# Making the Strassen sums of down's weights early, in DRAM

## The reference

```python
h = rmsnorm(x, mix_norm_g)
proj = h @ w_in                       # q, k, v (16 heads of 128) and 16 forget logits
q, k = rmsnorm(q, g_q), rmsnorm(k, g_k)
c = cumsum(log_sigmoid(f_logit + b_f))
logit[t, s] = q[t] . k[s] / sqrt(128) + c[t] - c[s]      # for s <= t
x = x + (softmax(logit) @ v) @ w_out
h = rmsnorm(x, ffn_norm_g)
gate, up = split(h @ w_gate_up)       # 2 x 5632 columns
x = x + (silu(gate) * up) @ w_down    # 5632 x 2048
```

## Time and profile before

| | before |
|---|---|
| median of 3 runs | 2136.73 us (2135.73 to 2136.99) |
| the profiled execution | 2136.44 us, span of its records 2134.7 us |
| PE busy | 2113.3 us (99%) |
| DVE busy | 1526.2 us (71%) |
| ACT busy | 944.6 us (44%) |
| DMA | 376.31 MB, 176 GB/s over the span |

### The profile page before, as it was taken

One profiled execution on the slowest core, in us unless ns is written; L12 is line 12 of the kernel. 1 busy time (PEld: TensorE's weight loads), 2 busy tenths in 40 slices (PEclk: granted clock), 3 DMA queues, 4 the chain that ended last, 5 costly groups with the idle time before them and its releaser, 6 DMA issues. The chain is left out here.

```text
span 2134.7 us, 27909 instructions
## 1 busy us (share of the span) xinstructions
PE 2113.3 (99%) x10404; PEld 1845.4 (86%) x10404; DVE 1526.2 (71%) x2108; ACT 944.6 (44%) x1281; POOL 174.2 (8%) x354
## 2 busy tenths in 40 slices
PE   8999999999999999999999999999999999999998
PEld 8999999999998888888888888888888777887876
DVE  4444444444455435888888987987978998999999
ACT  5333333333343335444444444544445554544533
POOL 0322222222221000000000000000000000000000
PEclk9999999999999999999999999999999999999999
DMA  6232333232243344666666666676677877868766
GB/s 185 76 99 79 93 85 92 79 98 79 84 128 128 119 134 132 198 218 200 219 212 211 208 219 212 204 233 204 198 235 232 269 256 246 263 208 269 260 186 203
DMA packets 258924, 376.31 MB, mean 176 GB/s; under 512 B 15842, under 2 KB 114180, under 8 KB 258324
## 3 DMA queue, kind: packets, MB, share of 16 engines
q1 hardware_dynamic: 255456, 354.90, 52.8%
q10 hardware_dynamic: 3380, 20.21, 2.5%
HBM read 346.45 MB, written 28.61 MB: 176 GB/s over the span
## 5 line engine op out<-in xcount | busy, mean ns | idle before, releaser
L1391 DVE TENSOR_TENSOR f_lo<-f_raw,f_hi 128x1536 fp32r<-128x1536 f32 (+1 forms) x230 | 454.4, 1980 | 46.9 <-ACT f_hi L1020 31.4
L564 PE MATMUL gemm<-w_hi,act_t 128*128 128x384 f32 (+2 forms) x1280 | 450.7, 352 | 2.3 <-DVE w_lo L1207 2.3
L565 PE MATMUL gemm<-w_lo,act_t 128*128 128x384 f32 (+2 forms) x1280 | 443.9, 347 | 0.0
L566 PE MATMUL gemm<-w_hi,act_t 128*128 128x384 f32 (+2 forms) x1280 | 443.9, 347 | 0.0
L765 PE MATMUL gemm<-f_hi,a_form 128*128 128x512 f32 x1056 | 411.2, 389 | 0.0
L767 PE MATMUL gemm<-f_hi,a_form 128*128 128x512 f32 x1056 | 411.1, 389 | 0.0
L766 PE MATMUL gemm<-f_lo,a_form 128*128 128x512 f32 x1056 | 410.8, 389 | 0.0
L765 PE MATMUL aux<-f_hi,a_form 128*128 128x512 f32 x792 | 313.2, 395 | 6.7 <-DVE f_lo L1391 5.1
L1207 DVE TENSOR_TENSOR w_lo<-w_raw,w_hi 128x768 fp32r<-128x768 f32 (+1 forms) x160 | 160.7, 1008 | 208.5 <-ACT w_hi L862 208.5
L766 PE MATMUL aux<-f_lo,a_form 128*128 128x512 f32 x792 | 308.5, 390 | 0.0
L767 PE MATMUL aux<-f_hi,a_form 128*128 128x512 f32 x792 | 308.5, 390 | 0.0
(11 more groups left out here) (184 smaller groups left out, 2227.5 us busy)
## 6 DMA issues: line engine op xcount, KB each, us to landing
f_raw<-in_ffn_w_gate_up SPq DMA_DIRECT2D x264, 512.0 KB, 4.2
f_raw<-in_ffn_w_down SPq DMA_DIRECT2D x132, 512.0 KB, 4.8
w_raw<-in_fox_w_in SPq DMA_DIRECT2D x192, 256.0 KB, 3.3
f_raw<-in_ffn_w_gate_up SPq DMA_DIRECT2D x88, 256.0 KB, 4.0
w_raw<-in_fox_w_out SPq DMA_DIRECT2D x16, 1024.0 KB, 5.1
f_raw<-in_ffn_w_down SPq DMA_DIRECT2D x44, 256.0 KB, 4.9
a_raw<-forms_scratch SPq DMA_DIRECT2D x22, 512.0 KB, 6.6
forms_scratch<-fa_a ACTq DMA_DIRECT2D x11, 896.0 KB, 6.3
```

Of the source, the lines that this page charges most:

```text
L564: mm(out, a_hi, b_hi, start=first, stop=False)
L565: mm(out, a_hi, b_lo, start=False, stop=False)
L566: return mm(out, a_lo, b_hi, start=False, stop=last)
L1391: v.tensor_tensor(f_lo[:, n % 4, 0:3 + g], f_raw[:, n % 4, 0:3 + g], f32(f_hi[:, n % 3, 0:3 + g]), ALU.subtract).then_inc(f_lo_done, 1)
```

## The change

The four blocks of every g = 1 unit of down are now loaded in the heads stage, summed there by DVE and stored in a DRAM tensor `t_scratch`. In down the units load the finished sums, and DVE's three instructions are gone; ACT's `f_hi` then waits for the load alone.

Heads 2 to 12 (`PRE_FIRST` to `PRE_END` - 1, a `Fori` of their own) each handle four units u = 0 to 3 of 1 MB. They use two buffers: `pre_w` behind `w_hi` for u = 0 and 2, `pre_rows` in the last quarter of `rows` for u = 1 and 3. ACT issues the loads (two DMAs each) and the stores (one DMA). A load waits until the buffer's last store has landed, a store until DVE's sums are made, DVE's sums until both halves of the load have landed. `add_p1` in down has one more wait.

```diff
+        pre = [at("pre_w", AREA_W + 49152, [P, 4, CW]), at("pre_rows", AREA_S + 24576, [P, 4, CW])]
@@ SP, the loads of the FFN's units
-                else:
+                elif r < R_DOWN:
                     for half in range(2):
                         sp.dma_start(f_raw[:, s, 2 * half:2 * half + 2], src[:, half, :, col:col + CW])\
                             .then_inc(f_ld[s], 16)
+                else:
+                    if r == R_DOWN and j == 0:
+                        for b in range(2):
+                            sp.wait_ge(pre_stored[b], 16 + 16 * NSTEP)
+                    made = dram_t[PRE_FIRST + step // 2, step % 2, (r - R_DOWN) % 2]
+                    for half in range(2):
+                        sp.dma_start(f_raw[:, s, 2 * half:2 * half + 2], made[:, 2 * half:2 * half + 2])\
+                            .then_inc(f_ld[s], 16)
@@ ACT
+            def load_blocks(h, u):
+                act.wait_ge(pre_stored[u % 2], 32 * (h - PRE_FIRST) + 16 * (u // 2) + 16)
+                src = w_down_v[bass.ds(h - PRE_FIRST, 1), u // 2].rearrange("o p r c x -> (o p) r c x")
+                for r in range(2):
+                    act.dma_start(pre[u % 2][:, 2 * r:2 * r + 2], src[:, r, :, u % 2 * CW:(u % 2 + 1) * CW])\
+                        .then_inc(pre_ld[u % 2], 16)
+
+            def store_sums(h, u):
+                act.wait_ge(pre_step, 12 * (h - PRE_FIRST) + 3 * u + 3)
+                dst = dram_t[bass.ds(h, 1), u // 2, u % 2].rearrange("o p f x -> (o p) f x")
+                act.dma_start(dst, pre[u % 2][:]).then_inc(pre_stored[u % 2], 16)
@@ in_chunk on ACT, in the order of a slot s
+                    if sums and s in (0, 1, 8):
+                        load_blocks(h, {0: 0, 1: 1, 8: 2}[s])
                     ...
+                    if sums and s == 10:
+                        load_blocks(h, 3)
                     ...
+                    if sums and s in (5, 8, 13, 14):
+                        store_sums(h, {5: 0, 8: 1, 13: 2, 14: 3}[s])
@@ ACT, f_hi of a g = 1 unit
-                    act.wait_ge(t_step, 3 * T_COUNT[n] + 1)
+                    if r < R_DOWN:
+                        act.wait_ge(t_step, 3 * T_COUNT[n] + 1)
+                    else:
+                        act.wait_ge(f_ld[n % 4], LANDED[n])
@@ DVE
+            def pre_sums(h, u):
+                f = pre[u % 2]
+                dve.wait_ge(pre_ld[u % 2], 64 * (h - PRE_FIRST) + 32 * (u // 2) + 32)
+                ...
+                v.tensor_tensor(f[:, 0:2], f[:, 0:2], f[:, 1:4:2], ALU.add).then_inc(pre_step, 1)
+                ...
+                v.tensor_tensor(f[:, 3], f[:, 0], f[:, 3], ALU.add).then_inc(pre_step, 1)
+                ...
+                v.tensor_tensor(f[:, 2], f[:, 3], f[:, 2], ALU.add).then_inc(pre_step, 1)
@@ in_chunk on DVE, in slot s behind split_lo
+                    if sums and s in (4, 7, 11, 12):
+                        pre_sums(h, {4: 0, 7: 1, 11: 2, 12: 3}[s])
@@ DVE in down
-                sums = n + 2 < NU and UNITS[n + 2][1] == 1
+                sums = n + 2 < NU and UNITS[n + 2][1] == 1 and UNITS[n + 2][0] < R_DOWN
```

More of the change, by code:

```diff
@@ L91, in encoder_layer @@
     dram_forms = nc.dram_tensor("forms_scratch", (NSTEP, P, 7, HW), F32, kind="Internal").ap()
+    PRE_FIRST, PRE_END = 2, 2 + FF // CW
+    dram_t = nc.dram_tensor("t_scratch", (PRE_END, 2, 2, P, 4, CW), F32, kind="Internal").ap()
     dram_x1 = nc.dram_tensor("x1_scratch", (ND, P, NT, CW), F32, kind="Internal").ap()
@@ L238, in encoder_layer @@
         f_ld = [sem(f"f_loaded{s}") for s in range(4)]
+        pre_ld, pre_stored = [sem("pre_loaded0"), sem("pre_loaded1")], [sem("pre_stored0"), sem("pre_stored1")]
+        pre_step = sem("pre_step")
         t_step, f_hi_done, f_lo_done = sem("t_step"), sem("f_hi_done"), sem("f_lo_done")
@@ L319, in encoder_layer @@
         assert len(SPLIT_NTH) == 2 * NSTEP
+        w_down_v = w_down.rearrange("(g r i p) (c x) -> g i p r c x", r=2, i=2, p=P, c=2)
         block = ctx.enter_context(nc.Block())
@@ L385, in _ @@
             w_gu_v = w_gu.rearrange("(g r i p) (c x) -> g i p r c x", r=2, i=2, p=P, c=2)
-            w_down_v = w_down.rearrange("(g r i p) (c x) -> g i p r c x", r=2, i=2, p=P, c=2)
             def load_forms(b, g, j):
@@ L928, in heads_hi, with in_chunk @@
                              rows_flat[:, h0 * S:(h0 + n) * S], ACT.Copy).then_inc(oT_hi_done, 1)
-            def in_chunk(h, second=False, last=False):
+            def load_blocks(h, u):
[8 more added lines that the diff above has]
+                act.dma_start(dst, pre[u % 2][:]).then_inc(pre_stored[u % 2], 16)
+            def in_chunk(h, second=False, last=False, sums=False):
                 for s in range(16):
@@ L951, in in_chunk @@
                         prob_split(h - 1)
+                    if sums and s == 10:
+                        load_blocks(h, 3)
                     if s == (13 if second else 12):
+                        if not (second or sums):
+                            act.wait_ge(pre_stored[1], 16 + 16 * NSTEP)
                         out_read(h - 1)
+                    if sums and s in (5, 8, 13, 14):
+                        store_sums(h, {5: 0, 8: 1, 13: 2, 14: 3}[s])
                     if last and s in (6, 9, 13):
@@ L983, in _ @@
             in_chunk(1, second=True)
-            with act.Fori(2, NH - 1) as h:
+            for b in range(2):
+                act.sem_inc(pre_stored[b], 16)
+            with act.Fori(PRE_FIRST, PRE_END) as h:
+                in_chunk(h, sums=True)
+            with act.Fori(PRE_END, NH - 1) as h:
                 in_chunk(h)
@@ L1058, in weights_hi_rest @@
             def weights_hi_rest(n):
-                act.wait_ge(t_step, 3 * T_COUNT[n] + 3)
+                if UNITS[n][0] < R_DOWN:
+                    act.wait_ge(t_step, 3 * T_COUNT[n] + 3)
                 a.activation(f_hi[:, n % 3, 2:4], f_raw[:, n % 4, 2:4], ACT.Copy).then_inc(f_hi_done, 1)
@@ L1305, in log_forget, with in_chunk @@
                 v.tensor_tensor(logf_lo[:], logf[:], f32(logf_hi[:]), ALU.subtract).then_inc(logf_split, 1)
-            def in_chunk(h, second=False, last=False):
+            def pre_sums(h, u):
+                f = pre[u % 2]
+                dve.wait_ge(pre_ld[u % 2], 64 * (h - PRE_FIRST) + 32 * (u // 2) + 32)
+                on_its_own(dve)
+                v.tensor_tensor(f[:, 0:2], f[:, 0:2], f[:, 1:4:2], ALU.add).then_inc(pre_step, 1)
+                dve.wait_ge(pre_step, 12 * (h - PRE_FIRST) + 3 * u + 1)
+                on_its_own(dve)
+                v.tensor_tensor(f[:, 3], f[:, 0], f[:, 3], ALU.add).then_inc(pre_step, 1)
+                dve.wait_ge(pre_step, 12 * (h - PRE_FIRST) + 3 * u + 2)
+                on_its_own(dve)
+                v.tensor_tensor(f[:, 2], f[:, 3], f[:, 2], ALU.add).then_inc(pre_step, 1)
+            def in_chunk(h, second=False, last=False, sums=False):
                 for s in range(16):
@@ L1358, in _ @@
             in_chunk(1, second=True)
-            with dve.Fori(2, NH - 1) as h:
+            with dve.Fori(PRE_FIRST, PRE_END) as h:
+                in_chunk(h, sums=True)
+            with dve.Fori(PRE_END, NH - 1) as h:
                 in_chunk(h)
@@ L1524, in add_p1 @@
                 dve.wait_ge(p2_read, 2 * r + 2)
+                if r >= R_DOWN + 2:
+                    dve.wait_ge(x1_p2, r - R_DOWN - 1)
                 x1 = rows[:, n, 0:2]
```

## The result

| | before | changed |
|---|---|---|
| median of 4 runs each | 2136.86 us (2135.73 to 2137.97) | 2184.70 us (2181.75 to 2189.59) |
| profiled execution, span | 2136.44, 2134.7 us | 2181.75, 2180.0 us |
| a head, mean of heads 3 to 12 | 39.24 us | 44.11 us |
| end of the heads | 647.8 us | 702.5 us |
| down, first unit to its last product | 430.7 us | 422.3 us |

The changed kernel is slower by 2.27% (ratio 1.0227, 95% interval 1.0215 to 1.0239). I had said 2147 us and a range up to 2162. The direction and the place were right, the size was not: the heads lost 54.7 us instead of 19; down gave back 8.4 us (9 said). Down begins at 1694.4 us in the kernel before and at 1749.15 in the changed one.

A forecast was written before the change was run, and what follows sets the result against it. Heads were taken as bound by PE alone, down by PE with a little of DVE. 2136.4 - 9 (down) + 19 (eleven heads' waits) = 2146.4, stated as 2147 us; range 2129 to 2162.

The forecast's parts named there:

- X: End of unit 3's sums on DVE, put at 331.4; PE does not wait up to 329.7, so 1.7 us a head.
- the first half of the head: Heads: unit 3's store, unit 1's load and the sums of units 0 and 1 delay things there; charged 0.
- A: Heads: each landing is early enough for unit 3's sums to end by 329.7; faster, 2127.4 us; chance 0.23.
- B: Heads against down: a wait of 5 to 13 us cancels the 9 us gain; 2132 to 2141; chance 0.15.
- D: Down gains nothing because the load's landing was the true limit; 2155 us; chance 0.05.
- C: Heads: DMA is the bound, loads and stores each 2 us longer, PE waits 4 us a head; 2171; chance 0.07.
- PE's wait for `w_lo`: Heads: named as a sign that DMA is the bound there.
- step 2: Head's end, ACT: waits until unit 1's store, issued at 316.4, has landed; put at 323.3, between 322.3 and 324.2.
- step 3: Head's end: unit 3's load, two issues, 0.6 + 4.9 = 5.5 us, landing at 328.8.
- Step 4: Head's end, DVE: unit 3's sums take 2.6 us; PE then waits 1.7 us a head, 19 us, upper bound 64 us.
- the weight split's limit: Head's end, DVE: the next group's weight split has until 333.8 and was said not to be the limit.

The follow-up runs named there:

- e10: Changed kernel, but at a head's end DVE waits for unit 3's blocks without summing them: 2150.62 us, heads of 41.39 us.
- e6: Changed kernel, but heads sum two buffers loaded once, early loads and stores left out, down as before the change: 2146.84 us.
- e3: Changed kernel without DVE's sums in the heads; all DMAs and ACT's waits stay: 2136.78 us, heads of 39.71 us.
- e1: Changed kernel, but only units 0, 1 and 2 are summed in the heads, unit 3 in down: 2130.12 us, ratio 0.9965 to the kernel before.
- e5: Changed kernel, but only units 0 and 1 are summed in the heads, the others in down: 2131.54 us, ratio 0.9969 to the kernel before.
- e9: Changed kernel, but ACT issues unit 1's store before unit 2's load instead of behind it: 2156.49 us, heads of 41.91 us.
- e7: Changed kernel with all early work in the heads, but down ignores the result and sums its blocks itself as before: 2197.83 us.
- e8: Changed kernel with the same work and bytes in other slots, unit 3 summed in the next head: 2205.93 us, ratio 1.0322 to the kernel before.
- e4: Changed kernel with nothing early in the heads; down loads its blocks as before but leaves their sums out: 2128.16 us.
- e2: Changed kernel, but in heads 2 to 8 unit 3 has a third buffer, so its load awaits no store: 2172.67 us.

## Why the prediction was wrong

**Right: the place and the chain.** I had said that everything hangs on X, the end of unit 3's sums, and that 11.1 us lie between X and the end of the scaling of tile 3. Two rows of DVE in the changed kernel, the emptying of tile 0, which follows unit 3's last sum at once, and the scaling of tile 3 in the next head:

```profile
316.73 0.35 DVE L1261 SCALAR_TENSOR_TENSOR work_r<-gemm,rms_x,work_r 128x128 fp32r<-128x128 f32 x1
...
327.12 0.48 DVE L1296 TENSOR_SCALAR qk_raw<-qk_raw,fac_qk 128x128 f32<-128x128 f32 x2 [1.56 <-POOL fac_qk L518]
```

The sum ends some 0.1 us after the first row's start (as at 360.95 above), at 316.8; 327.12 + 0.48 - 316.8 = 10.8 us. PE's loss follows X: 2.9 us less before X gave 2.7 us (e10), and in each of the eleven heads of the changed kernel the next head begins 1.7 us after X (362.73 after 361.04 above), which is the prediction's 0.74 + 0.96 us for the weight split.

**Right: the free parts.** DVE's work (e6), the traffic by itself (e3, 0.5 us a head at most) and the first half of the head (slots 3 to 14 unchanged) cost what I charged, nothing. In down the sum said 9 us and 8.4 came, with DVE at 70% where I had 67%. Rivals A, B and D fall by the result. C is the nearest to the size, and its terms were better than mine: it had each load and each store 2 us longer, and they were 1.6 and 1.8. Its reason, traffic that fills the engines, isn't borne out. The store was as slow with three quarters of the early bytes (e1), and took half as long with no load ahead of it (e5), and with all the traffic but no DVE in the line the heads lost 0.5 us (e3). PE's wait for `w_lo`, which I had put down as a sign of C, tells nothing between C and my own case once X is late enough.

**Wrong: step 2, the landing of the store.** I put it 6.9 us after its issue, the middle between the earlier trace rows. ACT could go on 8.7 us after the issue (median of 11; the store itself landed after 8.5): 1.8 us more. The right row was on the page. The store of rows 10 landed 8.6 us after its own issue, and its situation, a 1 MB store right behind a 1 MB load, is that of step 2; but I counted its 9.0 us from the load's issue, although here 1.5 us lie between the two issues and not 0.4, and then averaged it with stores that had no load ahead of them. e9 shows what such a store costs: 5.4 us, near the 5.9 of rows 11.

**Wrong: step 3, the landing of the load.** I took 5.5 us, from loads of the FFN. From its first issue to the first sum it took 7.1 us (median of 11): 1.6 us more. Rows 9 are loads of gate and up's weights. The same blocks of `w_down`, loaded by the kernel before in down, took 6.3 us from the first issue to the second landing (median of 44), which would have been the nearer row. Why it is 7 us in the heads is not shown. The engines were at 0.83 there (266 GB/s), where the earlier trace rows had 0.31; but in e5, with half of the early bytes and a share of 0.62, unit 0's load, with nothing of ACT's ahead of it and only unit 1's load behind it, took 7.4 us (median of 11), and in e1 7.0. So it isn't the bytes of all four units that make it long. The Trainium skill, "DMA: Bandwidth & Descriptors", section "Anatomy of one DMA", has about 2 us and the bytes at 436 GB/s, and gives this for DMAs that GpSimd issues. As an estimate worked out from it the load would have been in after some 5 us; these loads are issued by ACT, none of unit 3 was in before 6.6 us, and the measurement decides.

**Step 4, small:** the sums took 2.9 us with the gaps between them, not 2.6.

**The sum again.** X comes 1.8 + 1.6 + 0.3 = 3.7 us later, less 0.3: the store was issued 342.22 - 318.52 = 23.7 us into the head, of which 2.2 are the longer slots 0 and 2, so at 21.5 and not at my 316.4 - 294.6 = 21.8. 1.7 + 3.4 = 5.1 us a head; the chain of 10.8 us instead of 11.1 makes it 4.8, and the mean of heads 3 to 12 is 44.11 - 39.24 = 4.87. With X so late the weight split's limit, X of 332.1, is passed as well, which I had ruled out. By this sum it does not add to the total: PE's first wait (slot 15, 2.6 us) is time that it no longer has to wait in slots 0 and 2 (1.6 and 0.6 us). In e10 slot 15 is only 0.2 us longer than before, and slots 0 and 2 still lose 1.3 and 0.7 us.

**The range was too narrow for a sum that is multiplied by eleven.** The upper bound worked out in step 4 was 64 us; I set it aside because its landing of 8.1 us was the longest of 176. But the landings of eleven heads are not eleven draws: the same transfers stand in the same order each time, and all were long.

**Open:** why a load of 1 MB takes 7 us in the heads, and why store and load take 0.2 us longer each in e7 than in the changed kernel. Whether four units can be hidden in some other arrangement of slots wasn't tried beyond e8; e4's single run lies 2 us under e1, no more than the runs spread.

## What to carry to other kernels

Idle time of an engine is not a place where a wait can go: eleven heads had room for 10.4 us of sums, and one wait for data ahead of a serial chain, with the sums behind it, cost 4.9 us in each. Put only work whose data is long there ahead of such a chain, find every chain of the loop first (e8 moved the wait from one into another), and take as little of the new work as gives the gain: half of the units gave 5.9 of some 9 us to be had. Price a transfer by a row in which the same transfer stands ahead of it in the same queue, counted from its own issue.

## What the runs showed of the hardware

- A transfer taken out of a wait can come back in the queue: with the wait for the store gone (e2), unit 3's load is issued 5.1 us sooner and takes 3.4 us longer.
- A store behind a load in the same queue: 8.6 us with it ahead (e1), 4.5 us without it (e5), 5.3 us when the store goes first (e9; issue to landing, medians of 11).
- In nine of the eleven heads 3 to 13 PE's clock fell around its wait. Windows of the changed kernel: a part of slot 0 behind the wait of 2.58 us shown above, the whole of that slot, and slot 0 of a head whose clock did not fall:

```profile
364.20:366.87 2.67, 2.56 (x11) 2.06 (x10) 1.66 (x9) 0.00 (x0) 1.98 (x5) 0.50 0.93 246
362.73:366.87 4.14, 4.03 (x17) 3.54 (x17) 2.23 (x14) 1.36 (x4) 3.00 (x7) 0.64 0.97 301
449.84:453.83 3.99, 2.78 (x16) 2.53 (x17) 2.23 (x14) 1.36 (x4) 2.84 (x7) 1.00 0.96 302
```

  A granted clock of 0.50 is 1.2 GHz, 1.00 is 2.4. Yet the whole slot 0 lasted 4.14 us in the one and 3.99 us in the other, with PE busy for 4.03 and 2.78 us: at half the clock PE used up time in which it would otherwise have waited for q and k. Part of the 15 us by which PE's busy time exceeds that of before, with the same 10404 matmuls, is this and no work.
